# Transposes of the triangular inverse moved from TensorE to VectorE's 32x32 block transpose, with value scaling on ScalarE and a mask on POOL

## The reference

```python
decay = jnp.exp(jnp.where(tril, gcum[..., :, None] - gcum[..., None, :], -jnp.inf))
kb = kc * bc[..., None]
a = jnp.where(strict, jnp.einsum('nbhid,nbhjd->nbhij', kb, kc) * decay, 0.0)
ia = a + jnp.eye(lc)
u = triangular_solve(ia, vc * bc[..., None], unit_diagonal=True)
w = triangular_solve(ia, kb * jnp.exp(gcum)[..., None], unit_diagonal=True)
qk = jnp.einsum('nbhid,nbhjd->nbhij', qc, kc) * decay
# per chunk: v_new = u - w s;  o = (q exp(g)) s + qk v_new;  s = s exp(g_last) + (k exp(g_last - g))^T v_new
```

## Time and profile before

| | |
|---|---|
| median of three runs | 1934.16 us |
| the profiled execution | 1934.25 us |
| its span | 1932.6 us |
| TensorE busy | 1904.9 us (99%) |
| VectorE busy | 1048.0 us (54%) |
| ScalarE busy | 748.8 us (39%) |
| POOL busy | 147.6 us (8%) |
| mean granted TensorE clock | 0.996 |

### The profile page before, as it was taken

One profiled execution on the slowest core, in us unless ns is written; L12 is line 12 of the kernel. 1 busy time (PEld: TensorE's weight loads), 2 busy tenths in 40 slices (PEclk: granted clock), 3 DMA queues, 4 the chain that ended last, 5 costly groups with the idle time before them and its releaser, 6 DMA issues.

```text
span 1932.6 us, 31678 instructions
## 1 busy us (share of the span) xinstructions
PE 1904.9 (99%) x9888; PEld 1618.1 (84%) x9888; DVE 1048.0 (54%) x2318; ACT 748.8 (39%) x1538; POOL 147.6 (8%) x252
## 2 busy tenths in 40 slices
PE   7999999999999999999999999999999999999997
PEld 6999998888888888888888888888888888888886
DVE  6555556777777775574444444433334444444455
ACT  4444445554455443353333333333333333333330
POOL 1111111111111110001111110000000000000000
PEclk9999999999999999999999999999999999999999
DMA  7555564343334335344444444334444444444541
GB/s 221 153 143 150 143 164 115 98 105 104 99 104 111 109 108 166 108 121 125 135 141 125 133 128 128 126 128 130 129 128 123 133 123 126 127 126 156 181 133 66
DMA packets 241444, 249.99 MB, mean 129 GB/s; under 512 B 26488, under 2 KB 159616, under 8 KB 240736
## 3 DMA queue, kind: packets, MB, share of 16 engines
q1 hardware_dynamic: 234192, 233.60, 42.4%
q0 software_dynamic: 7184, 15.52, 2.7%
HBM read 237.67 MB, written 11.35 MB: 129 GB/s over the span
## 4 chain that ended last, share of the span: by engine, by line
PE 97%; DVE 1%; ACT 0%; DMA 0%; issue 0%; SPq 0%; DVEq 0%; POOL 0%; ACTq 0%; POOLq 0%
PE bank L292 70%; PE bank L1936 8%; PE bank L1682 7%; PE bank L1798 2%; PE bank L1196 1%; PE bank L1178 1%; PE bank L1850 1%; PE bank L1172 1%; PE bank L1190 1%; PE bank L405 0%; PE bank L1209 0%; PE bank L1136 0%; DMA x_res<-in_x_prompt 0%; PE bank L1182 0%; PE bank L1238 0%
## 5 line engine op out<-in xcount | busy, mean ns | idle before, releaser
L268 DVE TENSOR_TENSOR w_lo<-raw,w_hi 128x512 fp32r<-128x512 f32 (+2 forms) x828 | 563.0, 688 | 624.9 <-ACT w_hi L263 618.0
L263 ACT ACTIVATE w_hi<-raw 128x512 fp32r<-128x512 f32 (+2 forms) x828 | 499.9, 615 | 737.3 <-PE bank L292 607.2
L292 PE MATMUL bank<-w_hi,aT_hi 128*128 128x512 f32 (+2 forms) x1776 | 700.1, 394 | 3.0 <-DVE aT_lo L420 1.6
L292 PE MATMUL bank<-w_hi,aT_lo 128*128 128x512 f32 (+2 forms) x1776 | 674.2, 380 | 0.0
L292 PE MATMUL bank<-w_lo,aT_hi 128*128 128x512 f32 (+2 forms) x1776 | 672.6, 379 | 0.0
L292 PEld LDWEIGHTS bank<-w_hi,aT_hi 128*128 128x128 f32 x1776 | 334.9, 189 | 58.7 <-issue 9.0
L292 PEld LDWEIGHTS bank<-w_hi,aT_lo 128*128 128x128 f32 x1776 | 334.1, 188 | 56.1
L292 PEld LDWEIGHTS bank<-w_lo,aT_hi 128*128 128x128 f32 x1776 | 335.3, 189 | 46.8
L292 PE MATMUL bank<-w_hi,hT_hi 128*128 128x512 f32 x288 | 112.3, 390 | 0.0
L292 PE MATMUL bank<-w_hi,hT_lo 128*128 128x512 f32 x288 | 112.1, 389 | 0.0
L292 PE MATMUL bank<-w_lo,hT_hi 128*128 128x512 f32 x288 | 112.0, 389 | 0.0
(11 more groups left out here) (353 smaller groups left out, 2031.2 us busy)
## 6 DMA issues: line engine op xcount, KB each, us to landing
raw<-in_ffn_w_gate SPq DMA_DIRECT2D x176, 256.0 KB, 2.7
raw<-in_ffn_w_up SPq DMA_DIRECT2D x176, 256.0 KB, 2.7
raw<-in_ffn_w_down SPq DMA_DIRECT2D x176, 256.0 KB, 3.1
raw<-in_w_in SPq DMA_DIRECT2D x128, 192.0 KB, 2.4
raw<-in_w_in SPq DMA_DIRECT2D x128, 128.0 KB, 2.2
raw<-in_w_in SPq DMA_DIRECT2D x256, 64.0 KB, 2.2
raw<-in_w_out SPq DMA_DIRECT2D x61, 256.0 KB, 3.2
work_b<-in_cache_fox_k POOLq DMA_DIRECT2D x8, 512.0 KB, 4.7
```

The lines of the kernel that those rows point to most:

```text
L263: nc.scalar.activation(w_hi[:, g % RING, 0:width], raw[:, g % RAW, 0:width], ACT.Copy).then_inc(sem("w_high"), 1)
L268: nc.vector.tensor_tensor(w_lo[:, g % RING, 0:width], raw[:, g % RAW, 0:width], w_hi[:, g % RING, 0:width], ALU.subtract).then_inc(sem("w_ ...
L292: last = nc.tensor.matmul(acc[t][:, 0:width], l[:, k0 + n, t * P:(t + 1) * P], r[:, g % RING, 0:width], start=(n == 0 and j == 0), stop=(n ...
```

## The change

- The 32x32 block transpose of VectorE replaces TensorE's transposes where the inverse is block diagonal with blocks of up to 32: U from T ahead of level 1, and T from U for levels 2 to 5. ScalarE's copies of these go. Level 6 keeps TensorE's transposes and ScalarE's copies.
- Levels move to slots 17, 20, 23, 26, 30, 33 (from 18, 21, 24, 28, 31, 34). The product S·k gets slot 32.
- `nv` is scaled on ScalarE, behind a new semaphore `g_nrs`; the root behind it moves from level 3 to level 4. The mask of `decT` moves to POOL, behind its copies. `silu(1)` and `tanh(1)` move to slot 9, the exponential of `decT` to slot 12, `tanh(2)` to slot 22; the convolution of kind 2 is spread over one more level, `silu(2)` goes to level 3 and the transposes of kind 2 to level 4.

```diff
+SQUARE = 32
-G_OWN = 32
-G_READ = 22
+G_OWN = 31
+G_READ = 21
-LEVEL_AT = (0, 18, 21, 24, 28, 31, 34)
+LEVEL_AT = (0, 17, 20, 23, 26, 30, 33)
@@ gdn_pe
-                    W("g_T1"), W("g_fall")
-                    nc.tensor.transpose(tl(b7, 0), T[:, 0, :], ident).then_inc(sem("g_U1a_ps"), 1)
-                    W("g_ke")
-                    for t in (1, 2):
-                        last = nc.tensor.transpose(tl(b6, t), T[:, t, :], ident)
-                    last.then_inc(sem("g_U1b_ps"), 1)
-                    yield 17
                     L("g_cv", 2, 3)
...
                         L("g_Ua", n, LEVELS)
+                        if n == 1:
+                            W("g_ke"), W("g_fall")
...
-                        if n > 1:
+                        if 1 << n > SQUARE:
                             nc.tensor.transpose(tl(b5, 1), U[:, 0, :], ident).then_inc(sem("g_Ta_ps"), 1)
...
-                        if n > 1:
+                        if 1 << n > SQUARE:
                             for t in range(1, n_tiles(n)):
                                 last = nc.tensor.transpose(b7[:, (t - 1) * P:t * P], U[:, t, :], ident)
...
-                        if n == 3:
+                        if n == 4:
                             L("g_cv", 3, 3)
...
                         if n == 5:
+                            yield LEVEL_AT[n] + 2
                             W("g_nv")
@@ gdn_act
                     nc.scalar.activation(dec[:], dec[:], ACT.Exp).then_inc(sem("g_dec"), 1)
+                    tanh(1)
...
+                    yield 12
                     W("g_fall")
                     nc.scalar.activation(decT[:], decT[:], ACT.Exp, scale=-1.0).then_inc(sem("g_decT"), 1)
-                    yield 12
-                    tanh(1)
                     yield 16
-                    W("g_U1a_ps")
-                    nc.scalar.activation(U[:, 0, :], tl(b7, 0), ACT.Copy).then_inc(sem("g_Ua"), 1)
-                    W("g_U1b_ps")
-                    nc.scalar.activation(U[:, 1:3, :], tiles(b6[:, P:TOK], 2), ACT.Copy).then_inc(sem("g_Ub"), 1)
-                    yield 17
                     squares(1, b5, qkdT)
-                    for n in range(2, LEVELS):
-                        yield LEVEL_AT[n]
-                        m = n_tiles(n)
-                        L("g_Ta_ps", n - 1, LEVELS - 2)
-                        nc.scalar.activation(T[:, 0, :], tl(b5, 1), ACT.Copy).then_inc(sem("g_Ta"), 1)
-                        L("g_Tb_ps", n - 1, LEVELS - 2)
-                        nc.scalar.activation(T[:, 1:m, :], tiles(b7[:, 0:(m - 1) * P], m - 1), ACT.Copy)\
-                            .then_inc(sem("g_Tb"), 1)
-                        if n == 2:
-                            yield LEVEL_AT[n] + 1
-                            tanh(2)
+                    yield LEVEL_AT[2] + 2
+                    tanh(2)
+                    yield LEVEL_AT[4] + 2
+                    L("g_tok_ps", 3, 3), W("g_nrs")
+                    for t in range(TT):
+                        last = nc.scalar.activation(nv[:, t, :], tl(b3, t), ACT.Copy, scale=nrs[:, t:t + 1])
+                    last.then_inc(sem("g_nv"), 1)
+                    yield LEVEL_AT[6]
+                    W("g_Ta_ps")
+                    nc.scalar.activation(T[:, 0, :], tl(b5, 1), ACT.Copy).then_inc(sem("g_Ta"), 1)
+                    W("g_Tb_ps")
+                    nc.scalar.activation(T[:, 1, :], b7[:, 0:P], ACT.Copy).then_inc(sem("g_Tb"), 1)
@@ gdn_dve
                     yield 9
+                    silu(1)
...
                         .then_inc(sem("g_T1"), 1)
+                    W("g_T1")
+                    V.transpose(U[:, 0, :], T[:, 0, :]).then_inc(sem("g_Ua"), 1)
+                    V.transpose(U[:, 1:3, :], T[:, 1:3, :]).then_inc(sem("g_Ub"), 1)
                     yield 12
-                    silu(1)
                     conv(2, range(1))
                     for n in range(1, LEVELS):
-                        yield LEVEL_AT[n] - (n == 1)
+                        yield LEVEL_AT[n]
...
+                        if 2 << n <= SQUARE:
+                            m = n_tiles(n + 1)
+                            L("g_Ua", n + 1, LEVELS)
+                            V.transpose(T[:, 0, :], U[:, 0, :]).then_inc(sem("g_Ta"), 1)
+                            L("g_Ub", n + 1, LEVELS)
+                            V.transpose(T[:, 1:m, :], U[:, 1:m, :]).then_inc(sem("g_Tb"), 1)
                         if n == 1:
-                            conv(2, range(1, TAP - 1))
+                            conv(2, range(1, 2))
                         if n == 2:
+                            conv(2, range(2, TAP - 1))
+                        if n == 3:
                             silu(2)
-                            W("g_decT")
-                            for to, m in ((slice(0, 2), C_LP), (slice(2, 3), C_LS)):
-                                x = decT[:, to, :]
-                                ins = V.tensor_tensor(x, x, cn[:, m:m + P]..., ALU.mult)
-                            ins.then_inc(sem("g_decTm"), 1)
-                        if n == 3:
+                        if n == 4:
                             rsqrt(nrs[:], nss[:, 1, :], npol[:], after)
-                            after(V.tensor_tensor(nrs..., nrs..., bhalf..., ALU.mult))
-                        if n == 4:
-                            L("g_tok_ps", 3, 3)
-                            for t in range(TT):
-                                ins = V.tensor_scalar(nv[:, t, :], tl(b3, t), nrs[:, t:t + 1], None, ALU.mult)
-                            ins.then_inc(sem("g_nv"), 1)
+                            V.tensor_tensor(nrs..., nrs..., bhalf..., ALU.mult).then_inc(sem("g_nrs"), 1)
                             L("g_ss", 2, 2)
...
                             V.tensor_tensor(qkdT[:], tiles(b4[:, P:4 * P]), decT[:], ALU.mult).then_inc(sem("g_qkdT"), 1)
+                            yield LEVEL_AT[n] + 2
                             W("g_ks_ps")
@@ gdn_pool
                         G.tensor_copy(by_parity(kqm[:, m, :]), of_parity(tl(x, 2))).then_inc(sem("g_kqm"), 1)
+                    W("g_decT")
+                    for to, m in ((slice(0, 2), C_LP), (slice(2, 3), C_LS)):
+                        x = decT[:, to, :]
+                        last = G.tensor_tensor(x, x, cn[:, m:m + P]..., ALU.mult)
+                    last.then_inc(sem("g_decTm"), 1)
                     W("g_v2")
```

More of the change, by code:

```diff
@@ L1430, in gdn_dve @@
                             .then_inc(sem("g_Ub"), 1)
+                        if 2 << n <= SQUARE:
[4 more added lines that the diff above has]
+                            V.transpose(T[:, 1:m, :], U[:, 1:m, :]).then_inc(sem("g_Tb"), 1)
                         if n == 1:
-                            conv(2, range(1, TAP - 1))
+                            conv(2, range(1, 2))
                         if n == 2:
+                            conv(2, range(2, TAP - 1))
+                        if n == 3:
                             silu(2)
-                            W("g_decT")
-                            for to, m in ((slice(0, 2), C_LP), (slice(2, 3), C_LS)):
-                                x = decT[:, to, :]
-                                ins = V.tensor_tensor(x, x, cn[:, m:m + P].unsqueeze(1).broadcast_to(
-                                    [P, to.stop - to.start, P]), ALU.mult)
-                            ins.then_inc(sem("g_decTm"), 1)
-                        if n == 3:
-                            rsqrt(nrs[:], nss[:, 1, :], npol[:], after)
-                            after(V.tensor_tensor(nrs[:].unsqueeze(2), nrs[:].unsqueeze(2), bhalf[:, :, bass.ds(h, 1)],
-                                                  ALU.mult))
-                        if n == 4:
-                            L("g_tok_ps", 3, 3)
-                            for t in range(TT):
-                                ins = V.tensor_scalar(nv[:, t, :], tl(b3, t), nrs[:, t:t + 1], None, ALU.mult)
-                            ins.then_inc(sem("g_nv"), 1)
+                        if n == 4:
+                            rsqrt(nrs[:], nss[:, 1, :], npol[:], after)
+                            V.tensor_tensor(nrs[:].unsqueeze(2), nrs[:].unsqueeze(2), bhalf[:, :, bass.ds(h, 1)],
+                                            ALU.mult).then_inc(sem("g_nrs"), 1)
                             L("g_ss", 2, 2)
@@ L1547, in gdn_pool @@
                         G.tensor_copy(by_parity(kqm[:, m, :]), of_parity(tl(x, 2))).then_inc(sem("g_kqm"), 1)
+                    W("g_decT")
+                    for to, m in ((slice(0, 2), C_LP), (slice(2, 3), C_LS)):
+                        x = decT[:, to, :]
+                        last = G.tensor_tensor(x, x, cn[:, m:m + P].unsqueeze(1).broadcast_to(
+                            [P, to.stop - to.start, P]), ALU.mult)
+                    last.then_inc(sem("g_decTm"), 1)
                     W("g_v2")
```

## The result

The kernel after takes 1939.05 us (median of nine runs, 1938.88 to 1940.36), the kernel before in the same session 1933.57 us. The ratio is 1.0029, with a 95% interval of 1.0019 to 1.0039: the change makes the kernel 0.3% slower, by 5.5 us. The forecast was 1939.8 us.

The account below looks back on a forecast made before the run. TensorE, busy 99% of the span, bounds the kernel. Per loop head -1.5 + 1.3 + 0.9 + 0.1 = +0.8 us, seven times 5.6, last head about 0: 1939.8 us, 0.3% slower, range 1926 to 1946.

Parts of the forecast that it names:

- What bounds the stage: Delta-rule heads: only removed TensorE work and TensorE's waits for VectorE or ScalarE move the time.
- Part 1: Levels 2 to 5 and slot 16: 13 transposes per head leave TensorE, saving 1.5 us per head.
- Part 2 and 3: Level 1: VectorE's transposes and POOL's mask make Z late, costing 1.3 us per loop head, 0.4 in the last.
- The split of piece 3: VectorE ahead of level 1: queued behind the transposes, ending near 387.5 where TensorE wants weights at 387.34, 0.2 late.
- the 0.2 to 0.3 that I named as a sign: Expected trace reading, in us, of a VectorE transpose of one tile.
- Part 4: Level 5: value scaling on ScalarE delays VectorE's split and Z, so TensorE waits 0.9 us in all 8 heads.
- The slot of S·k: Behind slot 32: switching from wide products to narrow ones and back costs about 0.1 us per head.
- The sum: Delta-rule stage: +0.8 us per loop head, seven times 5.6; last head about 0; total 1939.8 us.
- Only TensorE's work counts: Rival: VectorE is early enough at levels 1 and 5, all 13 transposes gained, 11 us, 1923; chance 0.12.
- Level 1 keeps pace: Rival: no price at level 1, only the value path is late; 9.5 us less, 1930; chance 0.13.
- the value path is in time: Rival: no wait at level 5, only level 1 is late; 8 x 0.9 less, 1932.6; chance 0.07.
- VectorE's transposes are dear: Rival: transposes at levels 1 and 4 cost twice the tile rate; 7 us more, 1947; chance 0.10.

Follow-up runs that it names:

- e3: Kernel after with the mask of decT back on VectorE, behind the silu of kind 2 at level 3; 1937.1 us, ratio 1.0017.
- e8: Kernel after with the two block transposes of level 1 issued twice on VectorE, the first pair unread; 1941.8 us, ratio 1.0041.
- e5: Kernel after with value scaling in slot 30, first convolution step of kind 2 behind level 1, decT mask on VectorE behind level 3; 1927.0 us, ratio 0.9963.
- e1: Kernel after with ScalarE's scaling of the values moved from slot 28 to slot 30; 1931.3 us, ratio 0.9988.
- e2: Kernel after with the first convolution step of kind 2 moved on VectorE from ahead of level 1 to behind it; 1936.85 us, ratio 1.0016.

## Why the prediction was right

**What bounds the stage** held: work taken from TensorE counts in full, and so does each wait for VectorE.

**Part 1** (1.5 us per head less). Level slots of 1.36 and 1.15 us in place of 1.69 and 1.35 give 1.06 us for ten transposes. From the end of triple 16 to level 1 it was 387.92 - 385.68 = 2.24 us with a triple more; it is 386.23 - 385.20 = 1.03. The difference less 0.69 for the triple is 0.52, where I had 0.40, since that triple has no narrow work in front of it now. So 1.6.

**Part 2 and 3** (1.3 us more in a loop head). Measured 1.22 at the first half and 0.14 at the second (389.53 - 388.81 = 0.72 to the next wide product, where level 2 needs 0.58): 1.36. The split of piece 3, forecast 0.2 late, is: from the other tiles' products to the next triple it is 386.97 - 386.44 = 0.53 us, where level 2 has 0.36. That is inside the 1.22, since Z comes later still. Inside, the transposes cost 0.56 by start times for 0.54, with the same wait of 0.03 before them. (The forecast's lower bound of 0.19 each doesn't follow from the eight operations in 1.65 us that it names, which give 0.21; nothing rests on it.)

The price taken from one-tile operations of other kinds was right for a kind of operation that the trace didn't have; the duration of one tile, 0.31, is just above the 0.2 to 0.3 that I named as a sign. The figure of the Trainium skill (VectorE: DVE Perf Modes, "The three transpose paths"), 311 ns for a 128x128 bf16 tile, agrees with the duration of an f32 tile here, 0.31. It is not what a tile adds to a line of work: 0.23, and 0.33 for two in one operation. The kernel is 5 us faster than the 1944 estimated from that figure.

POOL's slowing was 0.2 us, as I took it from the gating product, and e3 confirmed it alone. But here the size was right and the picture was not. I put the mask at about 1 us beside the transposes; it took 2.08, the transposes were not slowed, and the 0.2 us is the convolution step that the mask's end reaches. I scaled the mask from one row by its columns, and did not see that VectorE's work can lengthen POOL's pass too (0.99 us for 0.45 in e8).

In the last head the cost was 0.65 plus 0.1 (691.55 to 693.57 is 2.02, where 1.37 was due), not 0.4, which had no working of its own. There the making of T on VectorE reads 0.86 us for the 0.56 of the other heads, with POOL's copies beside it, and the convolution step 0.81. In e5, without the mask on POOL, T reads 0.85 again, so there it is the copies and not the mask.

```profile
689.75 0.86 DVE L1405 TENSOR_TENSOR g_T<-cn,early 128x384 f32<-128x384 f32 x1
```

**Part 4** (0.9 us more in all heads). Measured 0.96 plus 0.1 behind it. VectorE's idle time in its split, forecast 1.1, reads 1.42, since the root and the floor took less of the line than I summed. The terms themselves closed: from the first half of level 4's second product it takes 404.59 - 398.98 = 5.61 us for the 5.57 of the sum, and 4.65 were due without a wait (403.63) for 4.64.

**The slot of S·k** (0.1 us more) cost nothing. From the second product of level 5 to the first of level 6 it takes 3.04 us before the change, and in e1, where the wait is gone, 402.52 to 405.56, again 3.04.

**The sum.** -1.6 + 1.36 + 1.06 = +0.8 us for a loop head, as measured: 50.94 for 50.13, forecast 50.9. The last head costs 0.4 where I had 0: from slot 2 to the product of slot 36 it takes 37.11 us for 36.69. Seven and one make 6.1 us; the medians differ by 5.5. In the profiled executions the spans differ by 4.8, because the part ahead of the delta-rule stage was 1.4 us shorter in that of after (slot 2 of the first head at 322.03 for 323.4), which the change doesn't touch. So the size of the change and its two places are the forecast's; that the total came as near as 0.8 us is partly luck, since small misses (the S·k slot against the 0.1 behind level 5's wait, the last head against the stretch ahead of the stage) cancel.

**The rivals.** "Only TensorE's work counts" falls: there are sixteen waits. Its price was nearly right: with nearly all waits gone (e5) the kernel takes 1927, and the 0.5 to 0.7 us per head still waited for are the way to its 1923. "Level 1 keeps pace" (1930) and "the value path is in time" (1932.6) are what one would get by mending one of the two; the second was run (e1), 1931.3. The first was run only in part (e2, e3). "VectorE's transposes are dear" falls by the 0.23 us. The chance I gave to slower, 0.51, was low for a chain of rows that closed so well.

## What to carry to other kernels

Work moved from the bounding engine to one with idle time is a gain only if it fits where it is put: the second engine's busy share (77% here, and unchanged by the change) didn't show it; the length of its queue between two meeting points did. So for each meeting point count what is queued ahead of it on the helper, its routine work for other streams included, and compare with the time that the bounding engine needs from its last word to the next. A wait that is put into an engine which also feeds the main stream holds that stream too: moving ScalarE's scaling behind one of its weight splits was worth 7.7 us, two thirds of what the transposes had to give.

## What the runs showed of the hardware

Where a pass on POOL and a two-input operation of VectorE lay side by side, one of them was lengthened. POOL's two-input pass of 128x128 read 0.99 us with a weight split of VectorE beside it (after) and 0.45 with block transposes alone (e8). Of VectorE's two-input operations beside the mask the one was slowed that started while a pass was well under way: the convolution step, 0.82 us for 0.61 (after, e3), and the second split in e2, 0.95 for 0.69. One that started before or together with the pass was not: in the loop heads the making of T (385.11, the pass at 385.17) read 0.56 and the first split (386.27, the second pass at 386.25) 0.65, with the mask and without it (e3). With POOL's copies it went either way: in the last head of after the making of T read 0.86 us, in that of e3 it read 0.58 and POOL's second copy 0.64 in place of 0.29. These rows look as if the two took turns; that is a reading of them, and no run tested it by itself.

VectorE's block transposes beside the same pass were not slowed: 0.31 us for one tile and 0.40 for two, in all heads and with or without the mask.

TensorE's products that it had to wait for cost about 0.1 us beyond the wait: the second half starts 0.32 us behind the first in place of 0.22, and each waiting line shown reads 0.48 us where one without a wait reads 0.38.
